# Two-block kernel on one NeuronCore: a reordered entry, and PSUM copies and additions placed first in the block-product units

## The reference

```
# first block
h = x
sh1, sc1, gt1, sh2, sc2, gt2 = split(silu(c) @ w_ada + b_ada, 6)
u = rmsnorm(h) * g_mix * (1 + sc1) + sh1        # the entry
h = h + gt1 * mixer(u)                          # w_in product, S5 branch, attention, gates
u = rmsnorm(h) * g_ffn * (1 + sc2) + sh2
a, val = split(u @ w_up)                        # feed-forward stage, 2048 + 2048 columns
h = h + gt2 * ((silu(causal_conv3(a) + b_conv) * val) @ w_down)
x = rmsnorm(h) * g_final
# second block ("second stage")
p = rmsnorm_2(x) @ w_in_2                       # gates, u, v, z, xb, bg, cg, xc, ...
x = x + merged_branches(p) @ w_o;  out = rmsnorm_2(x) * final_g
```

## Time and profile before

| | |
|---|---|
| median of 3 runs | 1996.53 us (1995.04 to 1999.32) |
| profiled execution | 1995.31 us, span 1993.6 us |
| TensorE busy | 1971.0 us, 99% |
| VectorE, ScalarE, GpSimd busy | 1143.7, 668.1, 1319.6 us |
| granted TensorE clock, mean | 0.999 |

### The profile page before, as it was taken

The page is one execution under the profiler, slowest core; times in us unless marked ns, Lnnn a source line. Parts: engine busy times, 40 slices in busy tenths (PEclk is TensorE's granted clock), DMA queues, the critical chain, the costliest instruction groups (busy, mean ns, idle before and its releaser), DMA issues. The chain is left out here.

```text
span 1993.6 us, 26010 instructions
## 1 busy us (share of the span) xinstructions
PE 1971.0 (99%) x10105; PEld 1639.9 (82%) x10105; DVE 1143.7 (57%) x1363; ACT 668.1 (34%) x1115; POOL 1319.6 (66%) x795
## 2 busy tenths in 40 slices
PE   8999999999999999999999999999999999999998
PEld 6888888888888787888888898888788888888888
DVE  6962378767652676656575386722464554624554
ACT  5213233233421454444321145433434433211103
POOL 4647457655364459999746538877787888858650
PEclk9999999999999999999999999999999999999999
DMA  9645564563644213333664422333323323198332
GB/s 336 201 118 160 172 185 151 159 199 115 216 161 156 85 64 106 103 130 106 234 251 159 148 86 64 119 115 112 120 77 136 127 85 106 34 377 317 117 137 86
DMA packets 195979, 295.41 MB, mean 148 GB/s; under 512 B 15416, under 2 KB 147472, under 8 KB 195856
## 3 DMA queue, kind: packets, MB, share of 16 engines
q1 hardware_dynamic: 185488, 270.55, 40.4%
q10 hardware_dynamic: 10368, 23.19, 3.1%
HBM read 213.73 MB, written 79.97 MB: 147 GB/s over the span
## 5 line engine op out<-in xcount | busy, mean ns | idle before, releaser
L1668 PE MATMUL ps<-tb,w_h 128*128 128x512 f32 x1344 | 416.9, 391 | 2.5 <-DVE quads L3056 1.9
L1052 POOL TENSOR_SCALAR w_h<-raw 128x512 fp32r<-128x512 f32 (+2 forms) x100 | 225.5, 2255 | 282.8 <-issue 127.1
L1173 POOL TENSOR_TENSOR w_l<-raw,w_h 128x512 fp32r<-128x512 f32 x210 | 309.5, 1483 | 92.6 <-ACT w_h L2307 92.6
L1668 PEld LDWEIGHTS ps<-tb,w_h 128*128 128x128 f32 x1344 | 251.3, 188 | 59.2 <-issue 3.9
L1668 PE MATMUL ps<-tb,w_l 128*128 128x512 f32 x672 | 261.5, 389 | 0.0
L2307 ACT ACTIVATE w_h<-raw 128x512 fp32r<-128x512 f32 x210 | 130.8, 627 | 236.8 <-PE ps L1668 150.3
L1668 PE MATMUL ps<-act_h,w_h 128*128 128x512 f32 x504 | 196.3, 389 | 0.6 <-ACT quads L2336 0.5
L1054 POOL TENSOR_TENSOR w_l<-raw,w_h 128x512 fp32r<-128x512 f32 (+2 forms) x100 | 191.3, 1913 | 8.3
L1668 PE MATMUL ps<-act_l,w_h 128*128 128x512 f32 x504 | 196.1, 389 | 0.0
L1668 PE MATMUL ps<-act_h,w_l 128*128 128x512 f32 x504 | 196.1, 389 | 0.0
L1668 PEld LDWEIGHTS ps<-tb,w_l 128*128 128x128 f32 x672 | 126.1, 188 | 26.3
(11 more groups left out here) (455 smaller groups left out, 4581.2 us busy)
## 6 DMA issues: line engine op xcount, KB each, us to landing
raw<-in_w_in SPq DMA_DIRECT2D x44, 1024.0 KB, 5.3
raw<-in_w_up SPq DMA_DIRECT2D x16, 1024.0 KB, 5.2
f_scratch<-r SPq DMA_DIRECT2D x16, 1024.0 KB, 8.3
gates_scratch<-quads SPq DMA_DIRECT2D x24, 512.0 KB, 7.6
r<-gates_scratch SPq DMA_DIRECT2D x12, 1024.0 KB, 6.4
ada_lo<-in_w_ada SPq DMA_DIRECT2D x16, 512.0 KB, 4.1
ada_hi<-in_w_ada SPq DMA_DIRECT2D x16, 512.0 KB, 4.4
gates_scratch<-gate_st ACTq DMA_DIRECT2D x32, 256.0 KB, 3.0
```

What stands on the lines that cost most here:

```text
L1052: nc.gpsimd.tensor_scalar(w_h[:, k, c, :], src[:, c, :], 1.0, None, ALU.mult).then_inc(s["w_high"], 1)
L1173: nc.gpsimd.tensor_tensor(w7_l[:, SLOTS[o]], x, w7_h[:, SLOTS[o]].bitcast(F32), ALU.subtract)\
L1668: last = nc.tensor.matmul(bank_of(n, bank), w[:, SLOTS[o], c, :], x(c), start=(first and c == 0 and p == 0), stop=(c == KD // 2 - 1 and p ...
```

## The change

In the entry, the root's table is loaded before the squares; `rows` are transposed and copied to columns ahead of x; GpSimd computes the angles before it splits the first weights; the diagonal product is issued in two halves with a semaphore of its own for the first; and h_t is divided by the root before the modulation is known. Gain and shift are then applied to the divided tile, by ScalarE for the high part and by VectorE (`tensor_scalar`) for the copy from which the low part is taken. "All eight tiles" are the eight channel blocks. In the units, `copies` and `from_first` are placed ahead of other work in the ScalarE and VectorE lists.

```diff
 # TensorE, entry
             for _ in range(8):
                 nc.tensor.matmul(slot(1)[:, 0:P], ident[:], ident[:], start=True, stop=True)
+            pe.wait_ge(s["vec_in"], 32)
+            nc.tensor.transpose(slot(3)[:, HALF:HALF + P], rows[:, 0, :], ident[:])
+            nc.tensor.transpose(slot(3)[:, HALF + P:HALF + P + n_b], rows[0:n_b, 1, :], ident[0:n_b, 0:n_b]).then_inc(s["colt"], 1)
             for t in range(QB):
...
-            pe.wait_ge(s["vec_in"], 32)
-            pe.wait_ge(s["h_ready"], QB)
-            nc.tensor.transpose(slot(3)[:, 0:P], rows[:, 0, :], ident[:])
-            nc.tensor.transpose(slot(3)[:, P:P + n_b], rows[0:n_b, 1, :], ident[0:n_b, 0:n_b]).then_inc(s["colt"], 1)
+            pe.wait_ge(s["h_ready"], QB - 1)
...
+            keep_busy(1)
+            ada_rows(0)
+            pe.wait_ge(*diag_first)
+            nc.tensor.matmul(slot(3)[:, 0:HALF], ones[:], diag[:, 0:4].rearrange("p b t -> p (b t)"), start=True, stop=True)\
+              .then_inc(s["head0"], 1)
+            everywhere(1, slot(3)[:, HALF:T], diag[:, 4:QB]).then_inc(s["rstd_ready"], 1)
+            ada_rows(1).then_inc(s["colt"], 1)
+            ada_columns(0)
             keep_busy(2)
-            ada_rows(0)
-            ada_rows(1).then_inc(s["colt"], 1)
...
-            spread[0]()
-            ada_columns(0)
-            spread[1]().then_inc(s["rstd_ready"], 1)
-            keep_busy(2)
...
-                         within={(0, 2): later_rows(1), (1, 0): later_columns(1), (2, 0): later_rows(2), (2, 2): later_columns(2),
-                                 (4, 0): later_rows(3), (4, 2): later_columns(3)})
+                         within={(0, 2): later_rows(1), (0, 3): later_columns(1), (2, 2): later_rows(2), (2, 3): later_columns(2),
+                                 (4, 0): later_rows(3), (4, 1): later_columns(3)})
 # VectorE, entry
-            on_diagonal(diag[:], stat[:, 1, :])
+            on_diagonal(diag[:, 0:4], stat[:, 1, 0:4], s["colt_read"])
+            on_diagonal(diag[:, 4:QB], stat[:, 1, 4:QB])
...
+            def divided(c, tok, done):
+
+                v.tensor_tensor(sq[:, c % 2, tok], h_t[:, c, tok], slot(3)[:, tok], ALU.mult).then_inc(done, 1)
...
+            divided(0, h0, s["head0"])
+            dve.wait_ge(s["rstd_ready"], 1)
+            divided(0, h1, s["t_ready"])
+            divided(1, slice(0, T), s["t_ready"])
             dve.wait_ge(s["c_ready"], 1)
             modulation_quarter(0)
...
+            def shifted(c, tok):
+
+                step(v.tensor_scalar(nrm[:, c % 2, tok], sq[:, c % 2, tok], gain[:, 0, c:c + 1], mod[:, c:c + 1], ALU.mult, ALU.add))
+
+            def rest_low(c, tok):
+
+                return v.tensor_tensor(act_l[:, c, tok], nrm[:, c % 2, tok], act_h[:, c, tok].bitcast(F32), ALU.subtract)
...
+            for q in range(1, 4):
+                for c in (2 * q, 2 * q + 1):
                     dve.wait_ge(s["u_ready"], c - 1)
+                    divided(c, slice(0, T), s["t_ready"])
                 modulation_quarter(q)
+                dve.wait_ge(s["t_ready"], 2 * q + 2)
                 for c in (2 * q, 2 * q + 1):
+                    shifted(c, slice(0, T))
+                    dve.wait_ge(s["hi_ready"], c + 1)
+                    rest_low(c, slice(0, T)).then_inc(s["u_ready"], 1)
 # GpSimd, entry
             pool.wait_ge(s["consts_ready"], CONSTS)
+            angles_of_the_states()
             pool.wait_ge(s["g_row_in"], 16)
             split_first()
-            angles_of_the_states()
 # ScalarE, feed-forward units
-                    if kind == "fa" and n > 4:
-                        for cg in range(2):
-                            f_high(p - 1, cg)
+                    if kind == "fv" and n > 1:
+                        copies(n, 0)
                     if kind == "fv":
                         for cg in (1, 0):
                             conv_first(p, cg)
-                    if n > 4 or n == 3:
-                        copies(n, 0)
+                    if kind == "fa":
+                        copies(n, 1)
...
-                    copies(n, 1)
+                    if kind == "fv":
+                        copies(n, 1)
...
+                if kind == "fv" and 5 < n < NF - 1:
+                    copies(n + 1, 0)
+                    f_high(p, 0)
                 if more:
                     weights_high(n + 1, 5)
+                if kind == "fv" and 5 < n < NF - 1:
+                    f_high(p, 1)
...
-                if n in (1, 3):
+                if n in (1, 3, 5):
                     f_high(p, 0)
                     copies(n + 1, 0)
                     f_high(p, 1)
 # ScalarE, second stage
             for t in range(4):
                 value_rows(1, t)
+                if t == 3:
+                    copies(NF, 0)
                 weights_high(NF, 3 + t)
...
+                if n > NF + 1:
+                    next_high(n, 0)
                 if n > NF:
-                    next_high(n, 0)
-                copies(n, 0)
-                if n == NF:
+                    copies(n, 0)
+                if n <= NF + 1:
                     next_high(n, 0)
 # VectorE, feed-forward units
-                elif n in (2, 4):
+                elif n in (2, 4, 6):
                     f_low(p - 1, 0)
                     from_first(n)
                     f_low(p - 1, 1)
                 elif kind == "fa":
+                    from_first(n)
                     for cg in range(2):
                         f_low(p - 1, cg)
+                else:
                     from_first(n)
-                else:
-                    if n == 1:
-                        from_first(n)
                     conv_rest(p, 1)
-                    if n > 1:
-                        from_first(n)
                     conv_rest(p, 0)
```

More of the change, by code:

```diff
@@ L2074, in root, with norm_high @@
                  .then_inc(s["std_ready"], 1)
-            def root_table():
-                A.activation(stat_e[:, 0, 0:1], eps_rms[:], ACT.Sqrt)
-            def norm_high(before, tok, buf, shift, after={}, first=None, place=None):
+            def norm_high(before, tok, buf, shift, after={}, first=None, place=None, gains=None):
                 for c in range(KD):
                     act.wait_ge(s["t_ready"], before + c + 1)
+                    if gains is not None:
+                        act.wait_ge(s["mod_ready"], c // 2 + 1)
                     dst, src = act_h[:, c, tok], buf(c)
@@ L2088, in norm_high @@
                         A.activation(place(c), src, ACT.Identity, bias=shift(c) if shift else 0.0)
-                    A.activation(dst, src, ACT.Identity, bias=shift(c) if shift else 0.0).then_inc(s["hi_ready"], 1)
+                    A.activation(dst, src, ACT.Identity, bias=shift(c) if shift else 0.0,
+                                 scale=gains[:, c:c + 1] if gains is not None else 1.0)\
+                     .then_inc(s["hi_ready"], 1)
                     if c in after:
@@ L2703, in scaled @@
-            def scaled(c, tok=slice(0, T)):
-                if c > 1:
-                    dve.wait_ge(s["u_ready"], c - 1)
-                v.scalar_tensor_tensor(nrm[:, c % 2, tok], h_t[:, c, tok], gain[:, 0, c:c + 1], slot(3)[:, tok],
-                                       ALU.mult, ALU.mult).then_inc(s["t_ready"], 1)
-            def low(c, tok=slice(0, T)):
-                dve.wait_ge(s["hi_ready"], c + 1)
-                v.scalar_tensor_tensor(act_l[:, c, tok], nrm[:, c % 2, tok], mod[:, c:c + 1], act_h[:, c, tok].bitcast(F32),
-                                       ALU.add, ALU.subtract).then_inc(s["u_ready"], 1)
@@ new lines, in _ @@
+            shifted(0, h0)
+            shifted(0, h1)
+            dve.wait_ge(s["head0"], 3)
+            rest_low(0, h0).then_inc(s["head0"], 1)
+            dve.wait_ge(s["hi_ready"], 1)
+            rest_low(0, h1).then_inc(s["u_ready"], 1)
+            shifted(1, slice(0, T))
+            dve.wait_ge(s["hi_ready"], 2)
+            rest_low(1, slice(0, T)).then_inc(s["u_ready"], 1)
+            dve.wait_ge(s["head0"], 4)
+            for q in range(1, 4):
+                for c in (2 * q, 2 * q + 1):
+                    dve.wait_ge(s["u_ready"], c - 1)
+                    divided(c, slice(0, T), s["t_ready"])
@@ L2724, in _ @@
                 modulation_quarter(q)
+                dve.wait_ge(s["t_ready"], 2 * q + 2)
                 for c in (2 * q, 2 * q + 1):
-                    scaled(c)
-                for c in (2 * q, 2 * q + 1):
-                    low(c)
+                    shifted(c, slice(0, T))
+                    dve.wait_ge(s["hi_ready"], c + 1)
+                    rest_low(c, slice(0, T)).then_inc(s["u_ready"], 1)
             dve.wait_ge(s["s5_act"], S5_ACT["turn_ready"])
```

52 lines of the change are left out of this document (22 added, 30 removed).

## The result

The changed kernel takes 2001.40 us (median of 11 runs, 1999.86 to 2002.29); the kernel before, timed beside it, 1994.36 (11 runs). The ratio is 1.0027, interval 1.0019 to 1.0035: slower by 7.0 us, where 1993.2 was forecast, 3.3 us faster, with a range of 1991.0 to 1998.5. The profiled execution spans 1999.0 us, where that of the kernel before spans 1993.6: in the two profiles 5.4 us are to be explained.

What follows compares the result with a forecast made beforehand. The prediction took TensorE to bound the kernel. Gains of 1.2 (entry), 1.15 (feed-forward) and 0.95 us (second stage) made 3.3 off the profiled 1995.31: 1992.0, or 1993.2 against the median; range 1991.0 to 1998.5.

Steps and rivals of the forecast that it cites:

- The start of the entry: Entry: TensorE starts the first large product at 26.0 instead of 27.25 us, a gain of 1.25 us.
- The rest of the entry: Entry's product: VectorE's three passes stall TensorE 0.4 us at tile 2; 0.4 of old waits goes; whole entry gains 1.2.
- the pattern which the prediction had found at tile 2: Entry, tile 2: VectorE reaches quarter 1's columns only after dividing tiles 2 and 3, a 0.4 us stall (0 to 1.5).
- the exclusion: VectorE instructions with two SBUF inputs and GpSimd instructions reading SBUF exclude each other; could raise units' stall to 1.5 us each.
- The units, what goes: Feed-forward units: three TensorE stalls (773.51, 788.50, 827.06) vanish through moved copies and additions, up to 2.55 us gained.
- The units, what comes: Feed-forward units 9, 11, 13: late sixth high part makes TensorE wait for GpSimd 0.3, 0.6, 0.5 us.
- Everything after these places follows TensorE, so a gain stays: Whole kernel behind the changed places: later work follows TensorE, so the 3.3 us gain is kept.
- The second stage: Second stage: two `from_first` stalls go, about 0.2 us comes back at unit 16, a gain of 0.95 us.
- (c): Rival: GpSimd bounds the feed-forward stage, TensorE loses 4.3 us at each of three units, 2004.7 us; chance 0.10.

Runs made afterwards that it cites:

- e11: The changed kernel with GpSimd's second weight split of the entry held until the eighth low part is done: 2002.50 us, ratio 1.0042.
- e4: The changed kernel with the next unit's sixth and seventh high parts back ahead of copy and `f_high` in units 7, 9, 11: 1996.43 us, ratio 1.0007.
- e5: The changed kernel; in unit 13 SyncE issues four scratch loads ahead of the down-weight load that waits for GpSimd: 1999.42 us, ratio 1.0019.
- e1: The kernel before with only the new ScalarE and VectorE orders of units 1 to 13: 2001.61 us, ratio 1.0031.
- e8: The changed kernel with the edits of e4, e5 and e6 together: 1992.05 us, ratio 0.9980.
- e9: e8 with low parts again TENSOR_TENSOR and SyncE's stores of r ahead of the weight load in units 6, 8, 10, 12: 1993.43 us, ratio 0.9996.
- e10: e9 with ScalarE's first convolution step of unit 13 ahead of the high part of its seventh weight piece: 1992.00 us, ratio 0.9984.
- e12: The units and second stage of e10 with the entry of the kernel before: 1989.63 us, ratio 0.9978.
- e7: The kernel before with only the move of SyncE's loads made in e5: 1995.43 us, ratio 0.9996.
- e6: The changed kernel with the entry's low parts as SCALAR_TENSOR_TENSOR instead of TENSOR_TENSOR: 2001.96 us, ratio 1.0029.

## Why the prediction was wrong

**The start of the entry: right.** 26.0 was forecast and 25.83 measured; part 2 of `w_ada` is used at 27.36, right at its forecast landing. The steps agree as well as the end: the first division starts at 20.46 (20.4 forecast) and the gain is done at 23.79 (23.9), so this is not luck. The angles took 9.3 us on GpSimd instead of 12, which changed nothing.

**The rest of the entry: a mis-sized term.** The low part was put at 1.22 to 1.70 us, a mean over many rows, and the sum divided that mean over the tiles. The low parts of the changed entry are not near their mean: 1.2 us for four of them, 1.94, 3.28 and 3.31 for the three that begin beside GpSimd's splits at 32.2, 35.5 and 51.9 (one of the four short ones, at 50.62, begins beside GpSimd's TENSOR_SCALAR too). Three waits come of it, each in its own way. At tile 2, 0.81 us (0.4 forecast, the place right): the shift takes 1.80 and the low part 1.94. At tile 7, 1.05 us: the low part takes 3.31. At tile 6, 0.72 us, the low part is short, but gain and high part begin only behind VectorE's two divisions, which end at 48.71; that is the pattern which the prediction had found at tile 2 and did not follow to tile 6. The 3.28 of tile 3 makes TensorE wait for nothing, it ends 1.0 us before it is wanted. The forecast has no wait at tiles 6 and 7; there it had let 0.4 go. Entry and first product together lost 1.0 us instead of gaining 1.2. The kernel before had one such low part too, beside the same split, at the same tiles:

```profile
50.30 4.62 DVE L2713 SCALAR_TENSOR_TENSOR act_l<-nrm,mod,act_h 128x1024 fp32r<-128x1024 f32 x2
```

4.62 for two, where two others take 2.48. It cost a wait of 0.3 us there, where VectorE has two passes a tile; that the third pass took the slack is likely, and no run shows it by itself.

The prediction cited the Trainium skill (SBUF — State Buffer, Who interferes with whom) for the exclusion, and used it for the units only. e11 agrees with it for the entry: 1.23 against 3.31 us. For the shift it weighed 0.99 from the single row against some 0.6 by the Trainium skill (VectorE: DVE Perf Modes, Mode 2×_2P). Undisturbed it took 0.81 here, between the two; the row of 0.99 had itself run beside GpSimd, at 1125.44 beside a TENSOR_SCALAR from 1124.39 to 1125.88.

**The units, what goes: right.** All three stalls went, and none of the moved copies and additions came late again.

**The units, what comes: the mechanism right, the size too small.** Waits at units 9, 11 and 13, for exactly the reason given (the late sixth high part): 0.49, 1.18 and 1.18 us, against 0.3, 0.6 and 0.5; with their restarts they took 3.5 us (252.1 against the 248.6 of e4, which removes them), where the sum has 1.4. The bounds of 0 to 2.2 a unit held; the value was taken at their lower end.

**"Everything after these places follows TensorE, so a gain stays": the step that failed.** The prediction followed the late high part to TensorE's next start, 1.4 us over three units, and stopped there. GpSimd's last low part of unit 13 has another reader: a load in SyncE's queue waits for it, and four loads stand behind that one. Counted from the start of unit 13 the low part came 5.9 us later than before, the cover was 0.6, and 5.05 us of waiting, 2.6 of low clock and 0.4 of restart make the +8.1 that the sum does not have. e5 shows the queue to be the cause of the wait, e1 that the units' order alone brings it. Behind it lay a second chain (store behind load, convolution behind high part, last rows, VectorE, TensorE) worth 3.4 us of waiting in e5, with a stretch of low clock behind it, and 2.9 us without one in e8, as soon as the first wait is taken away; e9 and e10 take it away in two steps.

**The second stage: right.** 0.95 was forecast; the traces have 1.1 in the changed kernel and in e12, 0.6 to 1.1 in seven others with the same code, and 0.0 in e10.

**The rivals.** (c), GpSimd as the bound, came nearest, on the slower side, but as it was written it did not happen: its price was 4.3 us at each of three units and its bound TensorE's wait for low parts, of which the changed kernel shows 1.2 at most and e5 1.8. The loss came where TensorE meets SyncE. The bounds of the prediction's own sum add up to a loss of 4.1 us, 2000.6 us; the range stopped at 1998.5, and neither holds 2001.4. A case "the late low part holds SyncE's queue" could have been priced from the trace before: the loads' issue, 11.9 to landing and 0.6 of cover.

## What to carry to other kernels

When a step on one engine is made later, follow everyone who waits for it, DMA queues above all: an in-order queue hands the delay to transfers that have nothing to do with it, and their cover, landing against first use, has to be read from the trace, since no table of waits shows a wait that does not yet exist. Order a queue so that what waits for the slowest engine stands last. And before stalls of the busiest engine are removed, ask whether it sets the end of the stage: here 2.55 us of stalls were slack that another chain needed, and were won only when that chain was shortened as well.

## What was not expected of the hardware

- Behind some pauses of TensorE the granted clock is at 0.50 for a while, with matmuls 0.43 us apart instead of 0.23, and behind others it is not. The length of the pause alone does not decide it. It fell with pauses of 5.05 us (the changed kernel, 990.5 to 997.4), 3.44 (e5, 1018.3 to 1021.7) and 1.77 (e9, 1013.7 to 1017.1). It stayed at 1.00 behind pauses of 2.94 (e8), 2.16 (e7), 1.76 (e5, unit 13) and 1.18 (units 11 and 13). Nor is the price fixed: from the down product's start to unit 14 the changed kernel loses 2.8 us and e11 1.4, behind the same pause of 5.0 us. So a shorter wait can cost more than a longer one: e9's stretch from unit 13 to unit 14 is 0.4 us longer than e8's.
- A VectorE operation with all its inputs in SBUF that begins while GpSimd's TENSOR_TENSOR runs is held until that one ends. In 128x1024, which takes 1.23 us alone, it ends 1.08 us behind it: 52.60 to 55.91 beside 51.85 to 54.83, 35.98 to 39.26 beside 35.48 to 38.18, and so do all the others of this size in the changed kernel that begin beside a TENSOR_TENSOR of 128x512 or more. TENSOR_TENSOR and SCALAR_TENSOR_TENSOR do not differ in it (e6). With one input from PSUM the same operations keep to 1.21 to 1.28 us beside it. Beside GpSimd's TENSOR_SCALAR they take between 1.21 and 2.06.
